# The four subtractions of each staged weight block: from VectorE, between its splits, to GpSimd

## What is computed

```python
h = _rmsnorm(x, norm1[l])
proj = jnp.einsum('bsd,de->bse', h, w_in[l])
(u_pool, c_b, c_c, c_x, q, k, v, qi, ki, wi, gate_logits) = jnp.split(proj, pts, axis=-1)
...  # pooling, short convolution, indexer-selected sparse attention: a, bconv, c
g = jax.nn.sigmoid(gate_logits...)
merged = (g[:, :, 0] * (a @ w_pool_out) + g[:, :, 1] * (bconv @ w_conv_out) + g[:, :, 2] * (c @ w_attn_out))
x = x + jnp.einsum('bsd,de->bse', merged, w_o[l])
h2 = _rmsnorm(x, norm2[l])
f = jnp.square(jax.nn.relu(jnp.einsum('bsd,df->bsf', h2, w_ff1[l])))
x = x + jnp.einsum('bsf,fd->bsd', f, w_ff2[l])
```

## Time and profile before

| | |
|---|---|
| median of 3 runs | 2655.76 us (2655.3 to 2656.8) |
| profiled execution: span from first to last instruction | 2654.2 us |
| TensorE busy | 2627.6 us, 99% |
| VectorE busy | 2015.7 us, 76% |
| ScalarE busy | 1241.8 us, 47% |
| GpSimd busy | 30.1 us, 1% |
| moved by DMA | 568.65 MB, mean 214 GB/s |

### The profile page before, as it was taken

One profiled execution on the slowest core, in us unless ns is written; L12 is line 12 of the kernel. 1 busy time (PEld: TensorE's weight loads), 2 busy tenths in 40 slices (PEclk: granted clock), 3 DMA queues, 4 the chain that ended last, 5 costly groups with the idle time before them and its releaser, 6 DMA issues.

```text
span 2654.2 us, 36222 instructions
## 1 busy us (share of the span) xinstructions
PE 2627.6 (99%) x14130; PEld 2256.9 (85%) x14130; DVE 2015.7 (76%) x2407; ACT 1241.8 (47%) x1614; POOL 30.1 (1%) x60
## 2 busy tenths in 40 slices
PE   8999999999999999999999999999999999999999
PEld 6688777777888888888889999999999788888887
DVE  4587756557777776676678888888887988888887
ACT  6322343335444544234556656656655433333333
POOL 0000000000000000000000000000000000000000
PEclk9999999999999999999999999999999999999999
DMA  7488775437455557856764565565568777685753
GB/s 242 141 272 285 266 243 177 160 109 240 166 175 180 169 174 255 285 197 212 254 229 146 188 219 193 181 223 174 200 222 302 277 261 262 214 317 176 273 191 121
DMA packets 321412, 568.65 MB, mean 214 GB/s; under 512 B 20000, under 2 KB 130208, under 8 KB 320736
## 3 DMA queue, kind: packets, MB, share of 16 engines
q1 hardware_dynamic: 290256, 463.53, 52.3%
q10 hardware_dynamic: 22928, 73.54, 7.5%
q0 software_dynamic: 8064, 29.36, 3.1%
HBM read 444.59 MB, written 121.63 MB: 213 GB/s over the span
## 4 chain that ended last, share of the span: by engine, by line
PE 86%; DVE 5%; DMA 5%; issue 1%; SPq 1%; ACT 1%; ACTq 0%; POOL 0%; DVEq 0%
PE aux L1242 8%; PE aux L1243 8%; PE aux L1244 8%; PE main L1346 8%; PE main L1348 8%; PE main L1347 8%; PE main L1242 6%; PE main L1243 6%; PE main L1244 6%; PE main L514 3%; PE main L516 3%; PE main L515 3%; DMA t_dram<-stage 1%; DMA stage<-w_o 1%; PE main L1277 1%
## 5 line engine op out<-in xcount | busy, mean ns | idle before, releaser
L1346 PE MATMUL main<-sf,f_wh 128*128 128x256 f32 x1728 | 489.2, 283 | 1.7 <-DVE cf_low L2806 1.4
L1347 PE MATMUL main<-sf,f_wh 128*128 128x256 f32 x1728 | 489.0, 283 | 0.0
L1348 PE MATMUL main<-sf,f_wl 128*128 128x256 f32 x1728 | 489.0, 283 | 0.0
L1346 PEld LDWEIGHTS main<-sf,f_wh 128*128 128x128 f32 x1728 | 331.8, 192 | 2.0 <-DVE cf_low L2806 1.6
L1347 PEld LDWEIGHTS main<-sf,f_wh 128*128 128x128 f32 x1728 | 331.8, 192 | 0.0
L1348 PEld LDWEIGHTS main<-sf,f_wl 128*128 128x128 f32 x1728 | 331.8, 192 | 0.0
L482 ACT ACTIVATE w_hi<-w_raw 128x512 fp32r<-128x512 f32 (+1 forms) x184 | 113.4, 617 | 275.5 <-PE main L516 211.6
L514 PE MATMUL main<-act_hi,w_hi 128*128 128x512 f32 x576 | 229.6, 399 | 8.2 <-DVE w_lo L489 7.2
L1514 ACT ACTIVATE f_wh<-group 128x1024 fp32r<-128x1024 f32 x128 | 135.8, 1061 | 200.7 <-PE aux L1244 105.3
L516 PE MATMUL main<-act_hi,w_lo 128*128 128x512 f32 x576 | 225.6, 392 | 0.0
L515 PE MATMUL main<-act_lo,w_hi 128*128 128x512 f32 x576 | 225.3, 391 | 0.0
(11 more groups left out here) (303 smaller groups left out, 5886.3 us busy)
## 6 DMA issues: line engine op xcount, KB each, us to landing
group<-w_ff SPq DMA_DIRECT2D x160, 512.0 KB, 5.1
f1raw<-w_ff SPq DMA_DIRECT2D x126, 512.0 KB, 5.7
sf<-f_dram ACTq DMA_DIRECT2D x56, 1024.0 KB, 11.4
group_g<-w_in SPq DMA_DIRECT2D x100, 512.0 KB, 4.5
w_raw<-w_in SPq DMA_DIRECT2D x87, 512.0 KB, 4.7
t_dram<-stage POOLq DMA_DIRECT2D x56, 512.0 KB, 4.6
f_dram<-piece_hi SPq DMA_DIRECT2D x112, 256.0 KB, 4.1
f_dram<-piece_lo SPq DMA_DIRECT2D x112, 256.0 KB, 5.2
```

Of the source, the lines that this page charges most:

```text
L1346: pe.matmul(part, hi_at(8, k)[:, cols], sh, start=first, stop=False, skip_group_check=True)
L1347: pe.matmul(part, hi_at(8, k)[:, cols], sl, start=False, stop=False, skip_group_check=True)
L1348: mm = pe.matmul(part, lo_at(8, k)[:, cols], sh, start=False, stop=last, skip_group_check=True)
```

## The change

GpSimd itself makes the four subtractions of each stage and then issues the four stores. mix_stage and its calls go away. In GpSimd's program the four subtractions of a stage stand together, behind a wait for the stage's loads; the stores stand behind the fourth. Before, each store was issued as soon as its sum was made. SyncE's queue, the buffers and the waits for stage_mixed and stage_stored elsewhere are the same.

```diff
-            def mix_stage(s, i):
-                b11, b12, b21, b22 = [block[:] for block in stage[stage_of(s)]]
-                if i == 0:
-                    dve.wait_ge(stage_landed, 64 * (s + 1))
-                    ins = dve.tensor_tensor(b11, b12, b11, ALU.subtract)
...
-                ins.then_inc(stage_mixed, 1)
...
             for n in range(8 * UP):
...
-                if n % UP >= 5:
-                    mix_stage(n // UP, n % UP - 5)
-                if n % UP == UP - 1:
-                    mix_stage(n // UP, 3)
...
-                if 9 <= n < 13:
-                    mix_stage(8, n - 9)
-                if 20 <= n < 24:
-                    mix_stage(9, n - 20)
-                if n >= 30:
-                    mix_stage(10, 2 * n - 60)
-                    mix_stage(10, 2 * n - 59)
...
-                if 8 <= n < 12:
-                    mix_stage(11, n - 8)
...
-                if g - u_b in (11, 12, 13, 14):
-                    mix_stage(12, (11, 12, 13, 14).index(g - u_b))
-                if g - u_b in (28, 29, 30, 32):
-                    mix_stage(13, (28, 29, 30, 32).index(g - u_b))
...
         def _(pool):
             for s in range(14):
-                g, h = s % 4, stage_of(s)
-                for i, b in enumerate((0, 1, 3, 2)):
-                    kind = (0, 2, 1, 3)[i]
+                g = s % 4
+                b11, b12, b21, b22 = [block[:] for block in stage[stage_of(s)]]
+                pool.wait_ge(stage_landed, 64 * (s + 1))
+                pool.tensor_tensor(b11, b12, b11, ALU.subtract).then_inc(stage_mixed, 1)
+                pool.wait_ge(stage_mixed, 4 * s + 1)
+                pool.tensor_tensor(b12, b22, b12, ALU.subtract).then_inc(stage_mixed, 1)
+                pool.tensor_tensor(b22, b22, b11, ALU.subtract).then_inc(stage_mixed, 1)
+                pool.wait_ge(stage_mixed, 4 * s + 3)
+                pool.tensor_tensor(b21, b21, b22, ALU.subtract).then_inc(stage_mixed, 1)
+                for i, block_i in enumerate((b11, b12, b22, b21)):
                     pool.wait_ge(stage_mixed, 4 * s + i + 1)
-                    pool.dma_start(t_dram[s // 4, kind, g]..., stage[h][b][:]
+                    pool.dma_start(t_dram[s // 4, (0, 2, 1, 3)[i], g]..., block_i
                                    ).then_inc(stage_stored, 16)
```

## The result

The changed kernel takes 2702.96 us (median of four, 2701.36 to 2706.77) against 2655.53 us (2655.3 to 2656.8): 1.0177 times as long, 95% interval 1.0163 to 1.0192, or 47.4 us more. The forecast was 2701, the range 2674 to 2724. The sum came within 2 us by luck: the stall of the ring was forecast some 21 us too long and the delays on VectorE at nothing, and the two errors cancel. The profiled run is the slowest of the four, 2706.77 us, with a span of 2705.0.

What follows compares the result with a forecast made beforehand. TensorE bounds the kernel, so relieving VectorE gives nothing. The profiled span of 2654.2 us, plus 45 of TensorE standing as stage loads come late, plus 1.6 from span to median, gives 2701 us, range 2674 to 2724.

Steps and rivals of the forecast that it cites:

- The ring: Stages 1 to 7, q and k: next stage load waits for stores, delaying w_raw loads; 28.8 us rounds, 45.2 us stall, 0.68.
- the joints: Three places between a stage's four subtractions where GpSimd and VectorE's splits get in each other's way: about 1.0 us a round.
- M: Time of one stage's four subtractions on GpSimd with waits between them: 11.0 us taken, 6.0 before, range 9.0 to 12.4.
- The lead: In q and k, how late load_stage(s) may come before TensorE stands: 16.6 us.
- The stores: Four stores issued together after the fourth subtraction: 8.5 us a round against 5.1; three held ones add 3.8 each, 11.4 us.
- Which the three units that are split ahead (8.2 us) hide: VectorE's splits delayed by up to one GpSimd subtraction each, 2.43 us, hidden unless TensorE already stands; nothing added.
- the later stages add nothing: Behind stage 7: stage loads lie further apart than a round, 1 us left out at stage 9, stages from 10 assumed to fit.
- gaps in the attention stretch with blocked splits as the cause: Sign that the forecast is wrong: TensorE's gaps lie elsewhere than in front of L514 between 180 and 350 us.
- Nothing changes: Rival: GpSimd subtracts about as fast as VectorE, below 1.3 us each, stall 4 us, 2660 us; chance 0.08.
- faster: Rival: VectorE's splits come earlier, 0.8 us, 2655; decides only if a round stays below 24.1 us; chance 0.02.
- The mild stall: Rival: subtractions of 1.6 to 1.9 us, or loads and stores 2 us shorter each round; 10 to 30 us; chance 0.15.
- VectorE becomes the bound: Rival: subtraction or mutual blocking above 2.6 us each overfills VectorE's round; 2714 us; both engines slowing, above 55 us: chance 0.07.

Runs made afterwards that it cites:

- five_apart: Changed kernel with a stage load behind every fifth w_raw load, not every fourth (stages 9 to 11 placed in the convolution columns): 2688.45 us, 1.0116.
- write_long: Changed kernel with each GpSimd subtraction replaced by two and a half zero fills, about as long but without reads, sums left out: 2679.61 us, 1.0088.
- late_only: Changed kernel with VectorE making the sums of stages 0 to 7 again and GpSimd only those of 8 to 13: 2672.33 us, 1.0050.
- late_write_long: Changed kernel with VectorE making the sums of stages 0 to 7 and GpSimd doing two and a half fills per sum in 8 to 13: 2657.58 us, 1.0004.
- half_columns: Changed kernel with each GpSimd subtraction on 512 of the 1024 columns, the other half of each sum left out: 2657.96 us, 1.0010.
- store_early: Changed kernel with each store issued right behind its own subtraction, all on GpSimd: 2691.50 us, 1.0119.
- write_only: Changed kernel with each GpSimd subtraction replaced by one zero fill, sums left out: 2653.56 us in a single run.

## Why the prediction came out right

That the time came out within 2 us of 2701 is luck, as two terms of the sum were wrong and cancel; that it is slower, and through the ring in the first place, is not.

**The ring: right.** The queue that waits for the stores and the w_raw loads behind it are as told; five_apart removes the lateness in q and k by the spacing alone. There are five gaps of the ring and not six, the first behind load_stage(3). The queue's wait for the stores, "some 60 us", came to 123.2. GpSimd's subtraction is 2.33 to 2.39 us where no split is under way as it begins, the first of each round (taken: 2.43), and 2.73 to 2.86 in the other three: the joints, put at 1.0 us a round, are some 1.2, and M is 10.8 where 11.0 stood. The load took 8.6 for 9.1. The price of the Trainium skill (GPSIMD Engine Reference, Performance versus the Vector engine), halved to an estimate of 2.25 us, lies below all of these rows. The lead was right too: load_stage(6) is 35.3 us late, less 16.6 is 18.7, and k ends 21.1 us late.

**The stores: a term of the sum mis-sized.** The seven rounds spend 56.7 us behind the fourth subtraction, 7.0 to 8.1 without a held store and 9.0 to 9.1 with one. The sum had 72.3 (8.7 and 12.5 with the wait for the signal). A held store adds some 1 to 2 us, not 3.8: while the fourth is held, the three before it drain, and it then lands alone in 2.90 us. So load_stage(7) is 40.5 us late and not 61.8, and by the prediction's own lead the stall would have been 23.9 us instead of 45.

| | predicted | measured |
|---|---|---|
| loads, seven rounds | 63.7 | 60.1 |
| M, seven rounds | 77.0 | 75.7 |
| stores and signals, seven rounds | 72.3 | 56.7 |
| load_stage(7) late | 61.8 | 40.5 |
| less the lead, 16.6 | 45.2 | 23.9 |
| lag where v begins | 45 | 35.9 |
| added behind that | 0 | 14.9 |

**"Which the three units that are split ahead (8.2 us) hide": the step that failed.** It priced one delayed split at a time and put the term at nothing. In q and k that holds (k ends 0.1 us late in five_apart); behind them it fails. The trace shows runs of delays: three instructions in a row that are needed by the same stretch of TensorE's work, 2.49, 2.85 and 2.88 us at 338 to 346 us for 0.69 each, together 6 us of delay, or four scalings at 470 us, 6.4 us. In the norms, the attention and the branches a chain runs from VectorE over ScalarE back to TensorE, and the cushion of split units isn't in it. So the same failure sits in the sentence that the later stages add nothing: their rings fit, as assumed, but fitting rings weren't the price. The prediction had named the sign of it, gaps in the attention stretch with blocked splits as the cause, and that sign came. Experiments size it: write_long, with a ring but no reads, costs 23.3 us; the other 24.1 of the 47.4 need the reads. Of these 5.0 us are a longer way to load_stage(7) (326.94 against 321.91), which leaves, as an estimate, some 19 for VectorE standing; some 14 of that lie in the late stages (late_only +14.9, late_write_long +1.3).

**The rivals.** "Nothing changes" and "faster" fell with the subtraction's length; half_columns, with rounds of some 23 us, agrees with the threshold of 24.1 us that the second named. The mild stall was right on the ring alone (10 to 30 us; 24 measured), and its reason was near: stores that take 2 us less in a round. "VectorE becomes the bound" was right on the mechanism, mutual standing, and wrong on the form: VectorE isn't full over a round (29 to 30 us busy in each 50), but it is while GpSimd subtracts (6.00 of 6 us from 340 to 346), and it delays by runs at places with no slack. Its condition, above 2.6 us each, holds in three subtractions of four (2.73 to 2.86). I had given the two of them 0.22 and each appeared in part.

The Trainium skill's rule on this was cited, and the forecast gave it one split at a time: a VectorE instruction with two SBUF operands and a GpSimd one that reads SBUF shut each other out for a whole instruction (SBUF — State Buffer, Who interferes with whom). The traces agree for VectorE's side, up to 2.9 us for a 0.69 us split against subtractions and 691 ns against fills, and for GpSimd's: 2.68 to 2.87 us where such an instruction is under way, 2.33 to 2.41 where none is. By the rule the prediction reckoned that every joint would let a whole split pass, M 12.1 and a stall of 53 us; a joint cost some 0.4 us, and M is 10.8. The clock behind the gaps, "not costed", does fall; see below.

## What to carry to other kernels

Work moved to another engine cost twice here: in the ring that it lengthens (here seven rounds by some 6 us beyond what TensorE gives, of which a lead of 16.6 us hides a part), and in what it does to the engine that it was taken from, which can end up busier than before. To part the two, run the moved work at the same length but without its reads. Price the delays where the receiving chain has no slack, and in runs, not one at a time. And when a wait is costed, ask which engine stands in it: a load 35.3 us late cost 21.1 where GpSimd waited for it, and one 21.5 us late cost 19.9 where VectorE did, with the splits behind it.

## What was not expected of the hardware

- A split that VectorE has ready during a subtraction on GpSimd ends some 0.5 us after that subtraction, so it takes up to 2.9 us for 0.69 (3.5 in store_early). Instructions with one tile as input are held as well (prob's scalings of 128x128, four in 7.58 us); the steps of the top-8 search (L2084, L2086) keep their length (685 and 676 ns for 128x512, 687 and 676 before). GpSimd is held in turn by a split under way: the second subtraction of half_columns takes 1.30 us at 169.16, with no split under way as it begins, the third 1.75 at 170.41, with one that began at 170.29.
- TensorE's granted clock was 1.00 in every stretch read before the change. In after it falls to the lower level, 1.2 GHz, behind all five gaps of 3.7 to 7.2 us and some of 2 to 3, and not behind the one of 1.8 at 281 us. Here TensorE had stood nearly the whole of 250 to 256 us:

```profile
250.00:256.00 6.00, 0.40 (x2) 0.00 (x0) 0.22 (x1) 0.96 (x2) 2.41 (x2) 0.97 1.07 367
256.00:262.00 6.00, 5.48 (x13) 4.32 (x14) 5.86 (x10) 1.34 (x3) 5.92 (x3) 0.50 0.43 138
```

The page's clock row, in tenths over slices of 68 us, shows nothing of it. The page's busy times bound what it is: the same 14130 matmuls keep TensorE busy for 2644.4 us instead of 2627.6, 16.8 of the profile's 50.8 us, and the other 34.0 are idle time. As a slow stretch before a load that comes late only takes the place of waiting, what the clock costs by itself stays open.
- The 8th, 15th, 22nd, 36th, 43rd and 50th of the 56 stores on GpSimd's queue are held, by 2.8 to 7.4 us in after, in bursts too; the 29th, the first of its burst, isn't. What holds them stays open.
- A fill of 128x1024 on GpSimd takes 0.96 us against 2.33 to 2.41 for a subtraction that isn't held, and two-operand instructions of VectorE keep their length beside it. prob's scalings, with one tile as input, don't quite: 382 ns on the mean for 128x128 in write_long, 287 before.
- Relieving VectorE of all 56 subtractions is worth some 2 us at most, even where nothing else is lost (write_only, a single run). No version was faster than the kernel before by more than its measurement can tell.
